# Attention and output projection in one program: output weights in the last head's buffers, last tile by column halves

## What is computed

```python
z = jnp.concatenate([attn * jax.nn.silu(ag), pool * jax.nn.silu(pg)], axis=-1)
y = x + gate[:, None, :] * (z @ w_out)
y_prompt, y_sample = rmsnorm(y over the prompt, final_g), rmsnorm(y over the sample, final_g)
```

## Time and profile before

| | us |
|---|---|
| median of three runs | 1360.7 (1356.75 to 1363.91) |
| the profiled execution | 1359.62 |
| its span in the trace | 1357.9 |
| mean granted TensorE clock | 0.968 of full |

### The profile page before, as it was taken

How to read it: one execution, slowest core, us unless ns; L and a number is a source line. 1 busy time by engine, 2 the same in 40 slices (tenths; PEclk the granted TensorE clock), 3 DMA queues, 4 the chain that set the end, 5 groups by cost and what they waited for, 6 DMA issues and landing times. The chain is left out here.

```text
span 1357.9 us, 19331 instructions
## 1 busy us (share of the span) xinstructions
PE 1277.6 (94%) x7007; PEld 1038.3 (76%) x7007; DVE 709.5 (52%) x1965; ACT 567.8 (42%) x1158; POOL 179.8 (13%) x196
## 2 busy tenths in 40 slices
PE   7899999999999999999699999999999992899996
PEld 1669988888888888888577777777777781788884
DVE  0646532343564211200088989989889882344444
ACT  2536521221121211111178878778788782201111
POOL 1223310101010010010000131041032042000000
PEclk9899999999999999999879999999999986899998
DMA  9636445022122444321295776959859126666663
GB/s 364 235 117 196 152 152 159 27 85 65 46 80 80 141 134 141 132 92 64 82 205 51 128 150 78 149 90 157 118 127 143 22 90 218 183 187 187 186 186 93
DMA packets 163836, 179.51 MB, mean 132 GB/s; under 512 B 35361, under 2 KB 125013, under 8 KB 159974
## 3 DMA queue, kind: packets, MB, share of 16 engines
q1 hardware_dynamic: 156990, 154.66, 45.9%
q10 hardware_dynamic: 6320, 22.05, 4.9%
q0 software_dynamic: 432, 1.57, 0.3%
HBM read 111.55 MB, written 66.69 MB: 131 GB/s over the span
## 5 line engine op out<-in xcount | busy, mean ns | idle before, releaser
L597 PE MATMUL prj_acc<-prj_hhi,til_whi 128*128 128x512 f32 (+1 forms) x800 | 286.3, 358 | 0.0
L599 PE MATMUL prj_acc<-prj_hlo,til_whi 128*128 128x512 f32 (+1 forms) x800 | 284.3, 355 | 0.0
L598 PE MATMUL prj_acc<-prj_hhi,til_wlo 128*128 128x512 f32 (+1 forms) x800 | 284.2, 355 | 0.0
L1467 DVE TENSOR_TENSOR att_wlo<-att_tps,att_whi 128x512 fp32r<-128x512 f32 (+1 forms) x336 | 185.7, 584 | 31.1 <-ACT att_whi L1438 28.2
L1438 ACT ACTIVATE att_whi<-att_tps 128x512 fp32r<-128x512 f32 (+1 forms) x336 | 164.8, 516 | 50.6 <-PE att_ops L1415 23.5
L599 PEld LDWEIGHTS prj_acc<-prj_hlo,til_whi 128*128 128x128 f32 x800 | 150.8, 188 | 21.4
L597 PEld LDWEIGHTS prj_acc<-prj_hhi,til_whi 128*128 128x128 f32 x800 | 150.9, 189 | 20.9
L598 PEld LDWEIGHTS prj_acc<-prj_hhi,til_wlo 128*128 128x128 f32 x800 | 150.8, 188 | 20.8
L1384 PE MATMUL att_sps<-att_ka,att_qa 128*128 128x512 f32 (+4 forms) x328 | 137.0, 418 | 14.4 <-DMA att_kb<-scratch_fkd 10.7
L1457 DVE TENSOR_SCALAR_CACHE_REDUCE att_wx<-att_sps 128x512 f32<-128x512 f32 (+4 forms) x164 | 94.0, 594 | 107.3 <-PE att_sps L1387 99.0
L1415 PE MATMUL att_ops<-att_whi,att_vt 128*128 128x512 f32 (+1 forms) x336 | 139.2, 419 | 0.0
(11 more groups left out here) (184 smaller groups left out, 1932.6 us busy)
## 6 DMA issues: line engine op xcount, KB each, us to landing
til_wraw<-in_w_in SPq DMA_DIRECT2D x20, 512.0 KB, 4.2
scratch_v<-val_vs SPq DMA_DIRECT2D x17, 512.0 KB, 4.5
val_xt<-in_x_prompt ACTq DMA_DIRECT2D x16, 512.0 KB, 4.3
ini_al<-in_w_ada SPq DMA_DIRECT2D x8, 1024.0 KB, 16.4
fin_zh<-scratch_z SPq DMA_DIRECT2D x16, 512.0 KB, 4.3
fin_zl<-scratch_z SPq DMA_DIRECT2D x16, 512.0 KB, 5.7
fin_x<-in_x_prompt SPq DMA_DIRECT2D x16, 512.0 KB, 5.7
out_y_prompt<-fin_o ACTq DMA_DIRECT2D x16, 512.0 KB, 5.7
```

What stands on the lines that cost most here:

```text
L597: pe.matmul(out, w[0][:, k, :], hhi[:, k, cs], start=(k == 0), stop=False)
L598: pe.matmul(out, w[1][:, k, :], hhi[:, k, cs], start=False, stop=False)
L599: mm = pe.matmul(out, w[0][:, k, :], hlo[:, k, cs], start=False, stop=(k == KT - 1))
L1467: dve.tensor_tensor(wlo[b][0:x.keys, x.skip:x.width], tps[x.i % T_RING][0:x.keys, x.skip:x.width], raw(whi[b][0:x.keys, x.skip:x.width]), ...
```

## The change

Attention and output become one program, `stage_finish`, with no barrier between them. `w_out` is loaded by SP at the place where a further head's queries and keys would be loaded (the last step of head 6), over head 6's query and key buffers. It is split in the same way, in eight slices, by new planner items `w_high` (ACT) and `w_low` (DVE), which can begin once the last score block of head 7 is done: the high part goes over head 7's query and key buffers, the low part over the raw weights. The two gate rows are loaded by SP over the even heads' values at the first step of head 7; z, the residual, `final_g` and a scratch `junk` lie in `wx`, `y` and `o` in `wy`, and the accumulators are the banks of `sps` and `tps`. `load_token` waits for the z of that tile's own gate rather than for all of them, so tiles 0 to 3 need gate 15 and only tiles 12 to 15 need gate 19, whose `gate_out` moves behind the loads of tiles 0 and 1. ACT's square writes into `junk`. Eviction and `finish` of a tile now follow each other directly. The last tile does all eight slices of its first 512 columns and then those of the second, with a semaphore for each half.

```diff
+W_OUT = [Slice(k) for k in range(KT)]
...
-    PRIORITY = {"PE": ("turn", "score", "value"), "ACT": ("out", "high", "exp"), "DVE": ("low", "add", "score", "den")}
+    PRIORITY = {"PE": ("turn", "score", "value"), "ACT": ("out", "high", "exp", "w_high"), "DVE": ("low", "add", "score", "den", "w_low")}
...
+        if kind == "w_high":
+            return at("score", BLOCKS[-1].i)
+        if kind == "w_low":
+            return at("w_high", x.i)
...
+        if kind in ("w_high", "w_low"):
+            return (930 if kind == "w_high" else 1130), 120
...
+        with Scope(nc, "raw") as a:
+            o_raw = a.sb("w", [P, KT, D])
+        with Scope(nc, "olo") as a:
+            o_lo = a.sb("w", [P, KT, D], F32R)
+        qa, qb, ka, kb = [None] * 2, [None] * 2, [None] * 2, [None] * 2
+        for e in range(2):
+            if e == 1:
+                with Scope(nc, "ohi") as a:
+                    o_hi = a.sb("w", [P, KT, D], F32R)
+            qa[e] = s.sb(f"qa{e}", [P, T], F32R)
+            qb[e] = s.sb(f"qb{e}", [KQ, T], F32R)
+            ka[e] = s.sb(f"ka{e}", [P, TC], F32R)
+            kb[e] = s.sb(f"kb{e}", [KQ, TC], F32R)
+        with Scope(nc, "gat") as a:
+            gate = a.sb("gate", [P, 2, D])
+            st_ = a.sb("st", [P, 6, NT])
         vt = [s.sb(f"vt{e}", [P, NQ + 2, P], F32R) for e in range(2)]
+        with Scope(nc, "zin") as a:
+            zh = [a.sb(f"zh{n}", [P, KT, P], F32R) for n in range(2)]
+            zl = [a.sb(f"zl{n}", [P, KT, P], F32R) for n in range(2)]
+            xr = a.sb("xr", [P, 2, D])
+            fg = a.sb("fg", [P, D])
+            junk = a.sb("junk", [P, D], BF16)
         wx = s.sb("wx", [P, 4 * SEQ])
+        with Scope(nc, "yo") as a:
+            y = a.sb("y", [P, 2, D])
+            o = a.sb("o", [P, 2, D])
...
+        acc = [[sps[0], sps[1]], [tps[0], tps[1]]]
...
+        def z_gate(t):
+
+            order = [out.q0 for out in OUTS if out.step.pair == PAIRS - 1 and out.step.e == 1]
+            return LAST + order.index(SEQ if t == NQ else 512 * (t // 4))
+
+        def load_token(sp, t):
+
+            b, n, c0, g = t % 2, W[t], t * P, z_gate(t)
+            if t >= 2:
+                sp.wait_ge(full1, t - 1)
+            sp.wait_ge(z_out[g % 2], 32 * (g // 2 + 1))
+            for part, (z, z_pair) in enumerate(((zh, 0), (zl, 1))):
+                sp.dma_start(raw(z[b][:, :, 0:n]), dram["z"][z_pair, :, :, c0:c0 + n].rearrange("k p c -> p k c")).then_inc(z_in[b], 16)
+            if t >= 2:
+                sp.wait_ge(yr, 2 * (t - 1))
+            sp.dma_start(xr[0:n, b, :], io["x_prompt"][0, c0:c0 + n, :] if t < NQ else io["x_sample"][0]).then_inc(x_in[b], 16)
...
-                elif at == 0 and 1 <= st.head < HEADS - 1:
+                elif at == NG - 1 and st.head + 2 == HEADS:
+                    sp.wait_ge(s_full, st.blocks[-1].i + 1)
+                    for n in range(2):
+                        k = slice(n * KT // 2, (n + 1) * KT // 2)
+                        sp.dma_start(o_raw[:, k, :], wv[:, k, :]).then_inc(w_in, 16)
+                elif at == 0 and st.head >= 1:
                     sp.wait_ge(val_ok, STEPS[st.index - 1].units[-1].i + 1)
-                    load_v(sp, st.head + 1)
+                    if st.head < HEADS - 1:
+                        load_v(sp, st.head + 1)
+                    else:
+                        for which in range(2):
+                            sp.dma_start(gate[:, which, :], dram["gate"][which].partition_broadcast(P)).then_inc(p_in, 16)
                 if st.e == 1:
                     gate_in(sp, st)
-            gate_out(sp, NS * PAIRS - 1)
+            sp.wait_ge(t_full, STEPS[-2].units[-1].i + 1)
+            for t in range(len(W)):
+                if t == 2:
+                    gate_out(sp, NS * PAIRS - 1)
+                load_token(sp, t)
+                if t == 0:
+                    sp.dma_start(fg[:, :], io["final_g"].partition_broadcast(P)).then_inc(fg_in, 16)
...
+            pe.wait_ge(s_free, NB)
+            pe.wait_ge(lo_ok, NU)
+            for t, n in enumerate(W):
+                b = t % 2
+                pe.wait_ge(z_in[b], 32 * (t // 2 + 1))
+                if t >= 2:
+                    pe.wait_ge(yg, 2 * (t - 1))
+                turns = [(k, (0, 1)) for k in range(KT)] if t < len(W) - 1 else [(k, (m,)) for m in range(2) for k in range(KT)]
+                for k, halves_ in turns:
+                    if t == 0:
+                        pe.wait_ge(w_lo, k + 1)
+                    for m in halves_:
+                        cols = slice(m * 512, (m + 1) * 512)
+                        out = acc[b][m][0:n, :]
+                        pe.matmul(out, zh[b][:, k, 0:n], o_hi[:, k, cols], start=(k == 0), stop=False)
+                        pe.matmul(out, zh[b][:, k, 0:n], o_lo[:, k, cols], start=False, stop=False)
+                        mm = pe.matmul(out, zl[b][:, k, 0:n], o_hi[:, k, cols], start=False, stop=(k == KT - 1))
+                        if k == KT - 1:
+                            mm.then_inc(full_h[m], 1)
...
+                if kind == "w_high":
+                    act.wait_ge(s_full, NB)
+                    act.wait_ge(w_in, 32)
+                    act.activation(o_hi[:, x.i, :], o_raw[:, x.i, :], ACT.Copy).then_inc(w_hi, 1)
+                    continue
...
+            for t, n in enumerate(W):
+                b = t % 2
+                act.wait_ge(yr, 2 * (t + 1))
+                if t >= 1:
+                    act.wait_ge(sq, t)
+                act.activation(junk[0:n, :], y[0:n, b, :], ACT.Square, accum_out=st_[0:n, 0, t:t + 1]).then_inc(sq, 1)
+                act.wait_ge(var, 2 * t + 2)
+                act.activation(st_[0:n, 3, t:t + 1], st_[0:n, 2, t:t + 1], ACT.Sqrt).then_inc(rs, 1)
+                act.wait_ge(o_ok, t + 1)
+                dst = io["y_prompt"][0, t * P:t * P + n, :] if t < NQ else io["y_sample"][0]
+                act.dma_start(dst, o[0:n, b, :]).then_inc(y_out[b], 16)
...
+                if kind == "w_low":
+                    dve.wait_ge(w_hi, x.i + 1)
+                    dve.tensor_tensor(o_lo[:, x.i, :], o_raw[:, x.i, :], raw(o_hi[:, x.i, :]), ALU.subtract).then_inc(w_lo, 1)
+                    continue
...
+            dve.wait_ge(p_in, 32)
+            for t, n in enumerate(W):
+                b = t % 2
+                which = 0 if t < NQ else 1
+                for m in range(2):
+                    cols = slice(m * 512, (m + 1) * 512)
+                    dve.wait_ge(full_h[m], t + 1)
+                    dve.tensor_tensor(y[0:n, b, cols], acc[b][m][0:n, :], gate[0:n, which, cols], ALU.mult).then_inc(yg, 1)
+                dve.wait_ge(x_in[b], 16 * (t // 2 + 1))
+                for m in range(2):
+                    cols = slice(m * 512, (m + 1) * 512)
+                    dve.wait_ge(yg, 2 * t + m + 1)
+                    dve.tensor_tensor(y[0:n, b, cols], y[0:n, b, cols], xr[0:n, b, cols], ALU.add).then_inc(yr, 1)
+                r = [st_[0:n, i, t:t + 1] for i in range(6)]
+                dve.wait_ge(sq, t + 1)
...
+                if t >= 2:
+                    dve.wait_ge(y_out[b], 16 * (t // 2))
+                dve.scalar_tensor_tensor(out=o[0:n, b, :], in0=y[0:n, b, :], scalar=r[4], in1=fg[0:n, :],
+                                         op0=ALU.mult, op1=ALU.mult).then_inc(o_ok, 1)
...
-        stage_attend(nc, io, keep, dram)
-        stage_out(nc, io, keep, dram)
+        stage_finish(nc, io, keep, dram)
```

More of the change, by code:

```diff
@@ L1124, with __init__ @@
     plan(_st)
+class Slice:
+    def __init__(self, k):
+        self.i = k
+W_OUT = [Slice(k) for k in range(KT)]
 S_RING, T_RING, W_RING, O_RING = 3, 3, 4, 2
@@ L1141, in __init__ @@
         self.order = {"PE": [], "ACT": [], "DVE": []}
-        self.tables = {"turn": UNITS, "value": UNITS, "high": UNITS, "low": UNITS, "out": OUTS, "add": OUTS, "exp": PIECES, "den": STEPS}
+        self.tables = {"turn": UNITS, "value": UNITS, "high": UNITS, "low": UNITS, "out": OUTS, "add": OUTS, "exp": PIECES, "den": STEPS,
+                       "w_high": W_OUT, "w_low": W_OUT}
     def at(self, what, i):
@@ L1249, in stage_attend @@
         v0_in = [s.sem(f"v0_in{c}") for c in range(4)]
+        names = ("w_in", "w_hi", "w_lo", "p_in", "fg_in", "full0", "full1", "yg", "yr", "sq", "var", "rs", "nr", "o_ok")
+        w_in, w_hi, w_lo, p_in, fg_in, full0, full1, yg, yr, sq, var, rs, nr, o_ok = (s.sem(f"f_{n}") for n in names)
+        z_in = [s.sem(f"z_in{n}") for n in range(2)]
+        x_in = [s.sem(f"x_in{n}") for n in range(2)]
+        y_out = [s.sem(f"y_out{n}") for n in range(2)]
+        full_h = (full0, full1)
+        acc = [[sps[0], sps[1]], [tps[0], tps[1]]]
+        W = [P] * NQ + [DEC]
+        wv = io["w_out"][0].rearrange("(k p) n -> p k n", p=P)
+        LAST = NS * (PAIRS - 1)
         FIRST_ROWS = [next(b.i for b in BLOCKS if b.row // 4 == c) for c in range(4)]
@@ L1446, in _ @@
```

(4 more changed lines are left out.)

143 lines of the change are left out of this document (13 added, 130 removed).

## The result

The changed kernel took 1338.7 us (median of four executions; 1337.3 to 1341.3) where the kernel before took 1358.7 beside it. The ratio is 0.985, with a 95% interval from 0.984 to 0.987: 20 us or 1.5% faster. The profiled execution took 1338.0 us, its span is 1336.3, against 1359.6 and 1357.9 before.

A forecast was written before the change was run, and what follows sets the result against it. TensorE was taken to bound attention's end and the output stage. First output product -20.9, clock -0.9, end -3.6, together -25.4 us: span 1332.5, profiled execution 1334.2, median 1335.3 us (chance 0.42); range 1327 to 1347.

The forecast's parts named there:

- two hand-overs: Into the output stage: attention ends on TensorE near 1135, and z allows the first output product at 1137.
- Attention's end: Last score block to last value product: the splits on ACT and DVE lengthen it by 6 us, to near 1135.
- The start of attention's end: TensorE's last score product of head 7, taken as staying at 1109.3.
- the pause in a rival: Near 1081 DVE stood 2.65 us; if open writes cause it, one more pause gives 1341 us; chance 0.06.
- SP's chain: SP's queue from step 21's sums to z: 7 us delay less 4.4 of slack, so 2.6 later; `gate_in` near 1091.
- my middle case: On SP's queue: `w_out` lands 4 us beyond 1069 and the gate rows add 2.7, taken as 7 us.
- my late one: SP's chain as one pair earlier: 10.0 us and 3, less 4.4, is +9; z at 1143, 1342.2 us; chance 0.20.
- The slack of 4.4 us: SP without work from 1097.9 to 1102.30 before the change; swallows 4.4 of the 7 us delay.
- The first output product: On TensorE, released by z: from 1157.9 to 1137, bounds 1132 and 1144; -20.9 us.
- Clock: Half clock at the output's start: loss falls from 1.9 to 1 us, as the gap is 2 us; gain 0.9.
- The end: Last product to span end: from 12.7 to 9.1 us, gain 3.6, bounds 3 and 4.
- The output's pitch: Output stage on TensorE: one product every 0.227 us, unchanged, with no waits between tiles.

The follow-up runs named there:

- experiment 11: The kernel of experiment 9 with the splits of `w_out` planned after attention's last low part: 1321.7 us, ratio 0.971 to the kernel before.
- experiment 8: The kernel before with the sums of step 21 written later, behind that step's fourth value unit: 1366.9 us (one timed run).
- experiment 7: The changed kernel with the last tile in the usual order, both column halves for each slice: 1341.3 us (one timed run).
- experiment 5: The changed kernel with loads of tiles 0 and 1 ahead of the last sums and the last gate's store before tile 4's loads: 1325.5 us, ratio 0.977.
- experiment 6: The changed kernel with sums written as one contiguous 16- or 32-byte piece per partition, landing in the wrong order: 1322.7 us (one timed run).
- experiment 9: The changed kernel with sums written in 16-byte pieces and read back in order by the first gate multiply: 1323.3 us, ratio 0.972 to the kernel before.
- experiment 10: The kernel before, without the merge, with sums in 16-byte pieces and the first gate multiply in written order: 1352.6 us, ratio 0.994.

## Why the prediction was right, and where it was not

The forecast was a median of 1335.3 us; it is 1338.7, within the range. The direction holds, and so does the frame of the mechanism: the output starts when the later of two hand-overs is there, and its length stays. Some of the steps within it do not hold:

- **Attention's end.** Forecast +6, and the last value product near 1135. Measured +5.0 and 1125.5. The term held, and experiment 11 shows that it is the splits: eight `w_high` on ScalarE between 1101.9 and 1121.7, `w_low` on VectorE until 1129.0. The place was 9.5 us off because of the row above it in the table. Part of the term was got by luck: I counted eight low parts of 1.16 us, 9.3 in all, and six stood before the last value product that took 9.0 us together, as beside GpSimd's gates one took up to 2.0 us.
- **The start of attention's end.** I held it fixed at 1109.3; it moved to 1101.4. This is the step that failed. From the second write of sums of step 21 to the last score block are 34.7 us in the changed kernel (from 1066.70) and 40.4 in the kernel before (from 1068.95): 5.7 us are the pause and the half clock of the earlier trace rows. The other 2.2 are a difference ahead of it, within the 4 us by which two executions of the changed kernel differ there. I had the pause in a rival as something that open writes cause, and asked only whether there would be a second one. With `w_out` ahead of them the pieces of step 21's write started only after 1080, where in the kernel before they had all started by 1071. Experiment 8 confirms the link between this write and the pause from the other side.
- **SP's chain.** Forecast `gate_in` of step 21 at 1091, measured 1092.1. The number was right in part by luck, and its reason wrong: counted from the sums of step 21 I had 15.3 + 7 = 22.3 us, and it took 25.8, about midway between my middle case and my late one; the sums themselves went out 2.2 us earlier, which hid part of it. I had 10.6 us for `w_out` at 395 GB/s from 1062 and 2.7 for the gate rows. In truth the load crawled at 31 GB/s for 9 us, ran at 407 for 9, and the sums waited behind it, as the earlier trace rows had shown. The 4% of the earlier trace rows, which I read as free engines, stood beside an open write of the same kind that then had nothing to slow. The slack of 4.4 us did swallow its part: the sums of step 22 went out at 1107.2, against 1105 by my sum. The rest of the chain, up to the first z load, took 23.6 us where I had 23.5.
- **The first output product.** Forecast 1137, measured 1139.4. `zl` was issued at 1131.2 where I had 1128.8, and landed after 8.2 us, where I had 7.7. The two hand-overs, however, did not fall together. I expected z to come 2 us after attention; it came 13.9 after.
- **Clock.** Forecast 1 us lost instead of 1.9. Measured: 12 products in 4.97 us where 21.9 fit, that is 9.9 x 0.227 = 2.2 lost. This follows from the line above: my gap of 2 us was one of 13.5, behind which the granted clock was 0.51, as after the 29 us of the kernel before.
- **The end.** Forecast 9.1 us, measured 9.15; but I gave 0.6 of the gain to the order by halves, and experiment 7 shows that this order does nothing. The semaphore for each half brings it by itself.
- **The output's pitch.** 806 products in 182.75 us, 0.227 each, unchanged, and no waits between tiles.

So the sum was 3.4 us short, and the largest miss did not enter it: the attention came 9.5 us earlier than I had it, of which z could use at most the 2.2 us of the earlier sums. By the rows, SP issued the sums of steps 22 and 23 straight behind its own z stores and did not wait for VectorE; so I estimate, and no run shows, that with the pause the time would still be about that of the late z. What is shown is that z set the start: experiments 5, 6 and 9, which make z early in three ways, each take 13 to 16 us off.

What stays open is how the writes of step 21 bring the pause about. Experiments 8 and 10 remove it by moving the write or widening its pieces, in one trace each, so it hangs on that write; that it is a refill of instructions caught behind it is not shown. The view of the DMA queues for 1074 to 1090 has one refill on queue 8 and one on queue 14, slower in the kernel before (first pair) than in the changed one (second pair):

```profile
q8 instruction: 1, 0.02, 1.5%
q14 instruction: 1, 0.01, 0.8%
```

```profile
q8 instruction: 1, 0.02, 0.4%
q14 instruction: 1, 0.01, 0.1%
```

These are 3.8 and 2.0 us of one engine, against 1.0 and 0.3 (16 x 16 us x the share). Only the one on queue 14 stands within the pause: the view for 1080 to 1084 has it and none of queue 8. Against the reading speaks experiment 8, in whose stretch from 1090 to 1098, with the moved write still open, both refills took over 2 us, and VectorE was busy for 7.86 of 8 us:

```profile
q8 instruction: 1, 0.02, 2.0%
q14 instruction: 1, 0.01, 1.8%
```

So a slow refill beside an open write is not enough for a pause. The Trainium skill (Runtime: NRT & Kernel Launch, Instruction fetch mechanics) calls the cost of a refill mostly hidden. The trace of experiment 8 agrees; whether the pause is an exception to it stays open.

## What to carry to other kernels

Look for writes in 4-byte pieces before costing any load that shares the DMA engines with them. Alone such a write leaves the engines nearly idle, so its own share does not give it away; beside a load a high DMA share with a low rate is its mark, and the load, here in pieces of 4 KB, is priced at that rate. When a stage is merged into the one before, follow the chain that releases its first input to its own end, on its own queue; here that chain was bound by three writes of at most 4 KB, and loading the first tiles ahead of the last of them, or widening them, brought 13 to 16 us beside the merge's 20. And an edit that only moves an engine's work from one side of a hand-over to the other can come out even, as the splits did.

## What the runs showed of the hardware

- An open write of sums in 4-byte pieces slows large packets beside it: 68 packets of `w_out` take 1.8 us each, the engines are 87% busy and move 31 GB/s. Once it is over a packet takes 0.13 us. Alone, such a write makes the engines 4% busy. In 16-byte pieces, with the same load, the stretch moves 357 GB/s. SP waits up to 11.6 us for such a write, and up to 4.3 for the wide one. The Trainium skill (DMA: Bandwidth & Descriptors, Rules for kernel authors) says that a non-contiguous last dimension becomes one descriptor per element and should be rearranged. The trace agrees, with 528 packets under 512 bytes for 512 sums, and adds that others pay: the load of `w_out`, which has no such pieces, crawled.
- SP can be stopped in the middle of an issue when a large load is queued ahead and a write in 4-byte pieces is open: 12.63 us at L1368. It takes 0.59 us with a quarter of the load, and 0.49 with the whole load and wide pieces (experiments 6 and 9).
- VectorE and GpSimd slow each other. In the timeline of the changed kernel a low part of `w_out` (both inputs in SBUF) takes 1.21 us alone and 1.65 beside a gate, and the gate's product 2.09 instead of 1.29:

```profile
1109.49 1.65 DVE L1571 TENSOR_TENSOR olo_w<-raw_w,ohi_w 128x1024 fp32r<-128x1024 f32 x1 [0.26 <-ACT ohi_w L1526]
...
1117.76 1.21 DVE L1571 TENSOR_TENSOR olo_w<-raw_w,ohi_w 128x1024 fp32r<-128x1024 f32 x1
```

```profile
1110.19 2.09 POOL L1658 TENSOR_TENSOR att_zhi<-att_ag,att_att 128x512 fp32r<-128x512 f32 x1
1112.23 1.29 POOL L1659 TENSOR_TENSOR att_rb<-att_ag,att_att 128x512 f32<-128x512 f32 x1
```

  The Trainium skill (SBUF — State Buffer, Who interferes with whom) says that a VectorE instruction with two SBUF inputs and a GpSimd instruction that reads SBUF lock one another out of a shared port. The trace agrees; I had not looked for it, and it was worth 0.3 to 0.8 us a low part in a stretch in which VectorE is the bound.
